# Pooling maps folded into the output projection, its bias summed from one load of its own, and five reorderings near the end of attention

## The reference

```python
# x: (1, 2048, 1024) float32; one layer
h = rms_norm(x, norm1_g)
q, k, v, p = split(h @ w_in)                 # 512 | 128 | 128 | 512 columns
a = sliding_window_sink_attention(rms_norm(q), rms_norm(k), v, sinks)   # chunks of 64, window 128
# pooling: 4 groups g of 128 channels, windows w = 2, 4, 8, 16
mixed_g = trailing_mean_w(p_g) - p_g
m_g = (mixed_g @ pool_w[g] + pool_b[g]) * pool_scale[g]
x = x + concat([a, m]) @ w_out               # rows 512..1023 of w_out meet m
x = x + conv_glu(rms_norm(x))                # up, causal conv(3), SiLU gate, down
```

## Time and profile before

| | us |
|---|---|
| median of 3 runs (lowest, highest) | 1776.46 (1774.86, 1777.26) |
| the profiled execution, own time | 1775.89 |
| its span, first to last instruction | 1774.1 |
| PE busy in the span | 1758.8 |
| DVE, ACT, POOL busy | 1334.1, 805.2, 245.4 |

### The profile page before, as it was taken

One profiled execution on the slowest core, in us unless ns is written; L12 is line 12 of the kernel. 1 busy time (PEld: TensorE's weight loads), 2 busy tenths in 40 slices (PEclk: granted clock), 3 DMA queues, 4 the chain that ended last, 5 costly groups with the idle time before them and its releaser, 6 DMA issues.

```text
span 1774.1 us, 23490 instructions
## 1 busy us (share of the span) xinstructions
PE 1758.8 (99%) x8518; PEld 1465.1 (83%) x8518; DVE 1334.1 (75%) x1794; ACT 805.2 (45%) x1437; POOL 245.4 (14%) x272
## 2 busy tenths in 40 slices
...
GB/s 326 228 214 107 123 323 89 167 296 154 171 162 184 196 84 126 136 84 95 119 250 213 72 83 96 71 84 95 72 83 253 334 341 329 307 255 218 297 285 131
DMA packets 211556, 321.75 MB, mean 181 GB/s; under 512 B 13737, under 2 KB 106097, under 8 KB 211441
## 3 DMA queue, kind: packets, MB, share of 16 engines
...
...
## 4 chain that ended last, share of the span: by engine, by line
PE 91%; DMA 3%; DVE 3%; ACT 2%; issue 1%; POOL 1%; ACTq 0%; SPq 0%; DVEq 0%
PE ps L827 29%; PE ps L828 29%; PE ps L829 29%; DMA raw<-in_w_in_dram 1%; PE ps L986 1%; PE ps L1010 1%; PE ps L997 1%; DMA raw<-in_w_out_dram 1%; PE ps L1050 1%; DMA gT_d<-cb 0%; DVE va_lo L1806 0%; DMA n<-in_x_dram 0%; POOL ss_q L2061 0%; PE ps L973 0%; ACT xs L1251 0%
## 5 line engine op out<-in xcount | busy, mean ns | idle before, releaser
L827 PE MATMUL ps<-va_hi,wv 128*128 128x512 f32 x1232 | 479.9, 390 | 1.8 <-DVE va_lo L1769 1.4
L829 PE MATMUL ps<-va_hi,wv 128*128 128x512 f32 x1232 | 479.3, 389 | 0.0
L828 PE MATMUL ps<-va_lo,wv 128*128 128x512 f32 x1232 | 479.3, 389 | 0.0
L827 PEld LDWEIGHTS ps<-va_hi,wv 128*128 128x128 f32 x1232 | 231.3, 188 | 51.7 <-issue 3.4
L829 PEld LDWEIGHTS ps<-va_hi,wv 128*128 128x128 f32 x1232 | 231.3, 188 | 48.2
L828 PEld LDWEIGHTS ps<-va_lo,wv 128*128 128x128 f32 x1232 | 231.3, 188 | 47.6
L827 PE MATMUL ps<-dt_hi,ds_hi 128*128 128x512 f32 x616 | 239.6, 389 | 0.0
L828 PE MATMUL ps<-dt_lo,ds_hi 128*128 128x512 f32 x616 | 239.6, 389 | 0.0
L829 PE MATMUL ps<-dt_hi,ds_lo 128*128 128x512 f32 x616 | 239.6, 389 | 0.0
L1856 DVE SCALAR_TENSOR_TENSOR cb<-ub,cst,cb 128x1024 f32<-128x1024 f32 x176 | 219.8, 1292 | 8.5 <-ACT cb L1377 8.5
L1377 ACT ACTIVATE cb<-ub,cst 128x1024 f32<-128x1024 f32 x88 | 109.1, 1244 | 142.3 <-DVE ub L1911 86.3
...
## 6 DMA issues: line engine op xcount, KB each, us to landing
...
rw<-in_w_up_dram SPq DMA_DIRECT2D x84, 512.0 KB, 5.0
...
gT_d<-cb ACTq DMA_DIRECT2D x44, 512.0 KB, 2.6
raw<-in_w_out_dram SPq DMA_DIRECT2D x32, 512.0 KB, 4.0
w_hi<-wA_d SPq DMA_DIRECT2D x30, 512.0 KB, 3.3
w_lo<-wA_d SPq DMA_DIRECT2D x30, 512.0 KB, 5.1
n<-in_x_dram SPq DMA_DIRECT2D x16, 512.0 KB, 8.2
```

The source lines that it names most:

```text
L827: pe.matmul(out_ap, l_hi, r_hi, start=first, stop=False, skip_group_check=True)
L828: pe.matmul(out_ap, l_hi, r_lo, start=False, stop=False, skip_group_check=True)
L829: return pe.matmul(out_ap, l_lo, r_hi, start=False, stop=last, skip_group_check=True)
```

## The change

- `pm` is gone from PE and ACT, and with it `mix_hi` and `mix_lo` from DVE. `mixed_g` goes straight to `join`.
- In block 0, `pwt` transposes the four `pool_w[g]` on PE; ACT and DVE scale and split them. Four stages `wp(h, pair)`, each with a 512 KB unit of `w_out`, multiply the folded map by it (6 matmuls a unit); ACT copies the products out and issues two 256 KB stores to `wP_d`. `o` with k < 2 loads its unit from there.
- The bias row: `bias_load` brings rows 512..1023 of `w_out` (2 MB) into `r`; POOL multiplies its four slices by pbias and adds them (`bias_sum`, 4 products and 3 sums of 128x1024); ACT and DVE split the sum (`bias_halves`); PE sums over the partitions with a matrix of ones (`bias`, 4 matmuls), ACT copies to `bias_all`. In every block POOL adds it to x (`rb`, 4 sums of 128x1024) ahead of DVE's addition.
- `r_load`: x for block 0 comes into the same `r`, so it now waits for the last `bias_sum`.
- Orders: in blocks 1 and 2 `sp(0)`, `t1(1)`, `sp(1)` in place of `sp(0)`, `sp(1)`, `t1(1)`; in block 3 `o(0, 1)` is cut in three pieces around `sp` and `av`, `o` and `va` are interleaved otherwise, `t2(2)` uses other banks; `V_ORDER` and `first_up` make half (0, i) before (1, i).

```diff
@@ attention_order, block 0 and the head of block 1
+        if not back:
+            units("pwt", a, ())
         units("q", a, (0,))
-        units("pm", a, (0,), (1,))
+        if a == 1:
+            units("r_load", a, ())
+            units("bias_halves", a, ())
         units("win", a, (2,))
...
         units("q", a, (2,))
-        units("pm", a, (2,))
+        if a == 1:
+            units("bias", a, ())
+        if not back:
+            units("wp", a, (0, 0))
         units("q", a, (3,))
...
             units("t1", a + 1, (0,))
-            units("pm", a, (3,))
+            units("wp", a, (0, 1))
             units("t1", a + 1, (1,))
+            units("bias_load", a, ())
             units("qn", a, ())
             units("pin", a + 1, (0,))
+            units("bias_sum", a, (0,), (1,))
...
             units("av", a, (0,), (1,))
+            units("wp", a, (1, 0))
...
             units("av", a, (2,), (3,))
+            units("wp", a, (1, 1))
+            units("bias_sum", a, (2,), (3,))
             units("kve", a + 1, ())
             continue
+        units("rb", a - 1, ())
         units("o", a - 1, (0, 0), (0, 1))
...
             units("t1", a + 1, (0,))
-            units("sp", a, (0,), (1,))
+            units("sp", a, (0,))
             units("t1", a + 1, (1,))
+            units("sp", a, (1,))
@@ attention_order, block 3
     units("av", last, (0,), (1,))
-    units("o", last, (0, 1))
+    units("piece", last, (0,))
     units("sp", last, (2,), (3,))
     units("pt", last, (2,), (3,))
     units("n2sc", last - 1, ())
+    units("piece", last, (1,))
     units("av", last, (2,), (3,))
+    units("o", last, (0, 1))
...
-    units("va", last, (1, 0), (0, 2))
+    units("va", last, (1, 0))
     units("o", last, (1, 1))
+    units("va", last, (0, 2), (1, 1), (1, 2))
+    units("o", last, (1, 2))
@@ SP
+            def r_load(a):
+                sp.wait_ge(S["bias_step"], 7)
+                sp.dma_start(r[:], x_v[:, 0:NT, :]).then_inc(r_in[0], 16)
+
+            def bias_load(a):
+                sp.wait_ge(const_ready, CONST_READY)
+                sp.wait_ge(S["mix_ready"], 4)
+                sp.wait_ge(S["fold_mm"], 1)
+                sp.dma_start(r[:], w_out_v[:, 4:8, :]).then_inc(r_in[0], 16)
@@ PE
+            def wp(a, n, h, pair):
...
+                for k in range(2):
+                    g = 2 * pair + k
+                    wait(pe, "fold_copied", 2 * (u - 1) + k + 1)
+                    mm = passes(ps[:, 4 + k, :], pw_hi[:, g, :], pw_lo[:, g, :], hi[:, k, :], lo[:, k, :], True, True)
+            def bias(a):
...
+                for h in range(2):
+                    pe.matmul(ps[:, 4 + h, :], ones[:], acc_hi[:, h, :], start=True, stop=False, skip_group_check=True)
+                    mm = pe.matmul(ps[:, 4 + h, :], ones[:], acc_lo[:, h, :], start=False, stop=True, skip_group_check=True)
@@ POOL
+            def bias_sum(a, g):
+                total = acc[:].rearrange("p h n -> p (h n)")
+                g_.tensor_tensor(r[:, g, :] if g else total, r[:, g, :], pbias[:, g:g + 1].broadcast_to([P, D]), ALU.mult
+                                 ).then_inc(S["bias_step"], 1)
+                if g:
+                    pool.wait_ge(S["bias_step"], 2 * g)
+                    g_.tensor_tensor(total, total, r[:, g, :], ALU.add).then_inc(S["bias_step"], 1)
+            def rb(a):
...
+                for t in range(NT):
+                    g_.tensor_tensor(rows[a][:, t, :], rows[a][:, t, :], bias_all[:].rearrange("p h n -> p (h n)"), ALU.add
+                                     ).then_inc(S["r_ready"], 1)
```

More of the change, by code:

```diff
@@ L30 @@
 ARENA = 20608
-RAW, RING, LEAD, MIX = 2, 3, 2, 2
+RAW, RING, LEAD, KEEP = 2, 3, 2, 4
 WARM = 28
@@ L171 @@
 ORDER = attention_order()
-UNIT_STAGES = ("pin", "kv", "q", "o")
+UNIT_STAGES = ("pin", "kv", "q", "wp", "o")
 UNIT = {}
@@ L185 @@
 N_SPLIT = len(SPLIT_NO)
-KEPT_UNITS = [n for n in SPLIT_NO if UNITS[n][0] != "o"]
+KEPT_UNITS = [n for n in SPLIT_NO if UNITS[n][0] not in ("wp", "o")]
 def first_unit(n):
@@ L731, in second_loads @@
                     load_vs(1, j)
-            walk(dict(pin=pin, kv=kv, q=q, o=o, first_loads=first_loads, second_loads=second_loads))
+            walk(dict(pin=pin, kv=kv, q=q, wp=wp, bias_load=bias_load, r_load=r_load, o=o, first_loads=first_loads, second_loads=second_loads))
             wait(sp, "v_lo", V_DONE[1, 4])
@@ L1012, in av, with piece, o @@
                 mm.then_inc(S["mix_done"], 1)
-            def o(a, n, h, k):
+            def piece(a, i):
+                o(a, UNIT["o", a, 0, 1], 0, 1, PIECES[i])
+            def o(a, n, h, k, part=None):
+                if part is None and (a, h, k) == (NB - 1, 0, 1):
+                    part = PIECES[2]
                 def tile_wait(t):
@@ L1056, in _ @@
             pe.wait_ge(const_pool, CONST_POOL)
-            walk(dict(t1=t1, pin=pin, pm=pm, kv=kv, q=q, kt=kt, qt=qt, s=s, sp=sp, av=av, o=o, t2=t2))
+            walk(dict(t1=t1, pin=pin, pwt=pwt, wp=wp, bias=bias, kv=kv, q=q, kt=kt, qt=qt, s=s, sp=sp, av=av, o=o, piece=piece, t2=t2))
             def up(un):
@@ L1197, in carry, with pwt, wp, bias_halves @@
                 a_.activation(p_keep[:, g, :], bank[:, T - CARRY:T], ACT.Copy).then_inc(S["p_copied"], 1)
-            def pm(a, g):
-                act.wait_ge(S["pool_done"], 4 * a + g + 1)
-                a_.activation(mf[:, g, :], ps[:, pm_bank(a, g), :], ACT.Identity, bias=pbias[:, g:g + 1],
-                              scale=pscale[:, g:g + 1]).then_inc(S["m_copied"], 1)
+            def pwt(a):
+                act.wait_ge(const_ready, CONST_READY)
+                act.wait_ge(S["fold_mm"], 1)
+                for g in range(4):
+                    a_.activation(pw_hi[:, g, :], ps[:, 4, tokens(g)], ACT.Copy, scale=pscale[:, g:g + 1]
+                                  ).then_inc(S["fold_hi"], 1)
+            def wp(a, n, h, pair):
+                u = folded(h, pair)
+                split(n + LEAD)
+                for k in range(2):
+                    i = 2 * u + k
+                    if k == 0:
+                        act.wait_ge(S["fold_mm"], u + 2)
+                    else:
+                        act.wait_ge(S["unit_used"], n + 1)
+                    if i == KEEP:
+                        act.wait_ge(S["fold_out"], 16 * KEEP)
+                    a_.activation(wp_kept[:, i % KEEP, :], ps[:, 4 + k, :], ACT.Copy).then_inc(S["fold_copied"], 1)
+                for k in range(2):
+                    i = 2 * u + k
+                    act.wait_ge(S["fold_copied"], i + 1)
+                    act.dma_start(wP_d[:, 2 * pair + k, h * 512:(h + 1) * 512], wp_kept[:, i % KEEP, :]
+                                  ).then_inc(S["fold_out"], 16)
+            def bias_halves(a):
+                act.wait_ge(S["bias_step"], 7)
+                act.wait_ge(S["fold_out"], 16 * 8)
+                a_.activation(acc_hi[:], acc[:], ACT.Copy).then_inc(S["fold_hi"], 1)
+            def bias(a):
+                act.wait_ge(S["fold_mm"], 6)
+                a_.activation(bias_all[:], ps[:, 4:6, :], ACT.Copy).then_inc(S["fold_copied"], 1)
             def kv(a, n, k):
@@ L1362, in va3 @@
                 v_hi(1, 3)
-            walk(dict(n1=n1_, n1sq=n1sq, t1=t1, pin=pin, pc=pc, pm=pm, kv=kv, kve=kve, q=q, kt=kt, qt=qt, s=s, pt=pt, av=av,
+            walk(dict(n1=n1_, n1sq=n1sq, t1=t1, pin=pin, pc=pc, pwt=pwt, wp=wp, bias_halves=bias_halves, bias=bias, kv=kv, kve=kve, q=q, kt=kt, qt=qt, s=s, pt=pt, av=av,
                       o=o, n2sq=n2sq, t2=t2, first_weights=first_weights, va=va, va3=va3))
```

167 lines of the change are left out of this document (97 added, 70 removed).

## The result

The changed kernel takes 1796.4 us (1793.7 to 1799.8), the kernel before 1776.5 in the same comparison: ratio 1.0116, 95% interval 1.0103 to 1.0129. The profiled execution took 1796.1, with a span of 1794.3 (from its first to its last instruction). The forecast was 1784.0, with a range up to 1790: the sign was right, the time is outside the range.

The account below looks back on a forecast made before the run. PE, busy 99% of the span, was taken to bound the kernel. The terms -8.2 + 1.1 + 0.9 + 2.2 + 0.4 + 12.6 + 1.6 - 1.0 - 2.1 gave +7.5, so 1784.0 us, range 1772 to 1790.

Parts of the forecast that it names:

- the stall of `q(1, 1)`: Block 1: PE waits for weights issued behind x, which waits for POOL's bias sums; +12.6, bounds 6 to 15.5.
- The lower clock behind it: Behind q(1, 1)'s stall: PE's clock falls and takes time to come back up; +1.6, 0 if it doesn't fall.
- B: At q(1, 1): weights overtake x or share the queue; stall 6 to 8 with its clock, about 1778; chance 0.15.
- C: At q(1, 1): SP's wait ends before PE gets there, so no stall; 1769.8; chance 0.13.
- the 36 matmuls: Blocks 1 to 3: pooling-map matmuls gone from PE where no wait covers them, 36 x 0.227 = -8.2.
- The -1.0 of `sp(1)`: Blocks 1 and 2: eight transposes of sp(1) between the last t1 and pin cover PE's 0.51 wait; -1.0.
- +2.2 ... POOL's first three bias operations ... +0.4: Block 0, pin(1, 0): weights land at 77.3, +2.2 (0 to 4); POOL beside join slows DVE, +0.4 (0 to 2).
- -2.1 (0 to -3.1): Block 3 and first up unit: new orders cover waits of 0.40, 0.67, 0.34 and 0.65.
- the 1.06: Wait at 528.76: goes, but PE waits instead for the next unit's first weights; counted as 0.
- the 0.65: First up unit: taking half (0, 4) first removes 0.65 of PE's wait.
- the sentence on `rb`: POOL's 16 bias sums end before DVE adds o's result: about 10 us of work, PE needs some 20.
- Rival D: Blocks 1 to 3: POOL's 23 added operations hold up DVE, two hits a block; +5, 1789; chance 0.12.

Follow-up runs that it names:

- e1: Changed kernel with block 0's 2 MB residual-row load issued behind the weights of q(1,1), q(1,2) and q(1,3) on SP's queue: 1781.8 us.
- e9: Changed kernel with all seven of POOL's bias-sum operations moved behind its last scaling of block 0's probabilities: 1788.6 us.
- e13: e11 with the fold's second unit, wp(0,1), moved from ahead of pin(1,0) to behind pin(1,2): 1778.7 us.
- e2: Changed kernel with the 2 MB bias_load issued behind pin(1,0)'s weights: 1792.4 us.
- e12: e11 with the bias cut to nearly nothing (128 KB load in place of 2 MB, sums and adds of 8 columns): 1773.2 us.
- e15: e11 with attention's last part in the order of the kernel before (o(3)'s third unit whole, va units, second loads, transposes' banks): 1774.0 us.
- e11: e10 with the four steps of the bias sum and block 3's four bias adds moved from POOL to DVE: 1773.3 us, ratio 0.9989 to the kernel before.
- e14: e11 with the changed kernel's order of the halves (V_ORDER and first_up): 1774.1 us.
- e7: e6 with POOL's bias adds on the residual rows cut from 1024 to 8 columns: 1775.5 us.
- e3: Changed kernel with POOL's four bias adds for block 3 done at the head of block 3, right behind those of block 2: 1793.4 us.
- e6: e5 with block 3's bias adds behind POOL's scaling of the first probabilities, not at the head of the block: 1784.6 us.
- e5: Changed kernel with both loads behind the weights, block 3's bias adds at its head, and first up unit's halves in the old order: 1778.6 us.
- e10: e5 with POOL's bias sums moved behind its last scaling of block 0's probabilities: 1776.1 us.

## Why the prediction was wrong

Stage by stage in the list: the prediction had +16.1 up to `o(0)`, -6.5 to `o(2)`, -2.1 from there, +7.5 in all. Measured: +21.6, -5.6 and +4.2 from there (2.3 up to the up stage, 1.5 in it, 0.5 in the down stage), +20.2. Of the 12.7 between them, 4.5 are at `pin(1, 0)`, 4.4 in block 3 and 2.0 behind it; the rest is in small terms. The two large ones are the steps that failed.

**Right: the stall of `q(1, 1)`.** SP's issue came 8.9 after POOL's copy began (9.3 forecast from `av`'s end), the four operations took 1.90, 2.40, 1.90 and 2.35 (1.9 and 2.4), the distance between the starts was 12.4, so 12.1 of stall beside the 12.6 forecast. The lower clock behind it cost 2.6 (1.6 forecast); together that is 14.7 (14.2 forecast), and e1 gives the same. Rivals B and C are out: the weights waited behind x, in e9 too.

**Right: the 36 matmuls.** Blocks 2 and 3 are 5.6 shorter up to `o(2)`, of which 24 x 0.227 = 5.4 are the maps. The -1.0 of `sp(1)` was 0.55: the distance of the two kernels' starts changes by 0.3 at `pin(2, 0)` (231.02 after, 209.70 before) and by 0.25 at `pin(3, 0)`. Another 0.3 was lost again in block 2.

**Failed: "+2.2 ... POOL's first three bias operations ... +0.4" at `pin(1, 0)`.** Measured +7.1 up to `pin(1, 1)` (87.05 before, 94.17 after), 4.7 by the wait and 2.4 behind it, where the two terms make 2.6. Three things were missed. The weights landed at 79.8, not 77.3, although SP issued `bias_load` at 62.9 and not 63.8: in the 16.9 us from there the DMA engines moved 5.7 MB at 337 GB/s, with 1.04 MB of ACT's stores among them, where the forecast had 4.2 MB and a part of 0.5 at 380. That is beyond the bound of 4. The clock halved behind this wait too (0.52 from 80 to 86), some 2.4, which I had charged to the other stall alone. And the weights would have been late without any bias: two more units in the ring of three moved `pin(1, 0)` behind q(0, 3)'s stores (issue at 67.5, in e13 at 65.5, before at 61.4). e2 shows 4.0 for the load with its clock, and e12 and e13 that the other 2.2 of wait are the ring's: they stay when the load shrinks to 128 KB, and go when a unit is moved.

**Failed: "-2.1 (0 to -3.1)" in the last half.** Measured +2.3 to the up stage, two mistakes in one term. The orders are worth 0.5 there, as e15 shows, and nothing beyond it: what they close in attention reopens at the first up unit, where in e11 the start distance is 1.1 too long and before it was 0.65, and what the halves' order closes in that unit comes back as the 1.66 of e14 (the prediction had seen that for the 1.06 and not for the 0.65). And the sentence on `rb`, that it "ends before DVE adds `o`'s result", answered the wrong question. It did end in time, but while it ran DVE's operations waited for it: +3.2 against e7, which has hardly any adds, and e11, where DVE makes them. e3, e6 and e7 together show that the adds and not the orders cost this, since moving or cutting them alone moves the time by 1.3 to 8.3.

**Rival D's mechanism was real.** It cost 3.2 here. It was priced in the wrong place (two hits in each of blocks 1 to 3) and taken as an alternative, where it comes on top of the forecast. In block 0 it was hidden by `pin(1, 0)`'s stall and in block 1 by `q(1, 1)`'s. When these were gone a wait of 1.7 (0.5 before) appeared in e5 and one of 1.5 in e1. e10 shows what made the first: the sums leave `join`, and it goes back to 0.5.

**Open.** The +1.5 between the up and the down stage lies within what the same stage shows over all kernels (844.5 to 846.5). Of the 2.5 between e5 and e10 the traces place 1.2, the wait for the softmax; e5's trace also began 2.1 late, so they can't place the rest. Nothing here shows why a wait of 2.2 lowers the clock in one execution and not in another.
